# A windowed-attention layer that divides its probabilities before they are transposed, with the sink as one more column of the score bank

## The reference

```python
s = where(valid, q @ k.T * scale, -inf)
m = maximum(max(s), sink)
p = exp(s - m)
p = p / (sum(p) + exp(sink - m))
o = p @ v                       # then oc = o * silu(gate), and out = oc @ w_out
```

## Time and profile before

| | |
|---|---|
| median of 3 runs | 1123.61 us (1123.01 to 1125.2) |
| the profiled execution, its own time | 1122.13 us |
| its span in the profile | 1120.3 us |
| mean granted clock of TensorE | 0.997 |
| PE busy | 1088.0 us, 97% of the span |
| DVE busy | 967.9 us, 86% |
| ACT busy | 679.0 us, 61% |
| DMA queue of SP | 102.87 MB, 33.5% of 16 engines |

### The profile page before, as it was taken

One profiled execution on the slowest core, in us unless ns is written; L12 is line 12 of the kernel. 1 busy time (PEld: TensorE's weight loads), 2 busy tenths in 40 slices (PEclk: granted clock), 3 DMA queues, 4 the chain that ended last, 5 costly groups with the idle time before them and its releaser, 6 DMA issues. The chain is left out here.

```text
span 1120.3 us, 18456 instructions
## 1 busy us (share of the span) xinstructions
PE 1088.0 (97%) x5672; PEld 907.7 (81%) x5672; DVE 967.9 (86%) x1955; ACT 679.0 (61%) x1310; POOL 0.2 (0%) x4
## 2 busy tenths in 40 slices
PE   7999999999999999999999999999999999999996
PEld 6778778878888888888888867787888888888875
DVE  5879889889889889889889898789888988988886
ACT  6475565565654654654654765366677666677764
POOL 0000000000000000000000000000000000000000
PEclk9999999999999999999999999999999999999998
DMA  7614423323324224225125120454332324323111
GB/s 230 167 41 108 137 76 77 112 75 90 98 75 101 86 75 116 71 75 130 57 75 146 43 75 28 117 146 107 102 94 56 94 60 120 103 75 94 57 38 76
DMA packets 131530, 103.67 MB, mean 93 GB/s; under 512 B 5408, under 2 KB 116384, under 8 KB 131488
## 3 DMA queue, kind: packets, MB, share of 16 engines
q1 hardware_dynamic: 131344, 102.87, 33.5%
q10 hardware_dynamic: 144, 0.26, 0.1%
HBM read 77.95 MB, written 2.10 MB: 71 GB/s over the span
## 5 line engine op out<-in xcount | busy, mean ns | idle before, releaser
L74 PE MATMUL bank_proj<-hH,w_hi 128*128 128x512 f32 x856 | 341.1, 398 | 1.9 <-DVE w_lo L1295 1.1
L76 PE MATMUL bank_proj<-hH,w_lo 128*128 128x512 f32 x856 | 334.3, 390 | 0.0
L75 PE MATMUL bank_proj<-hL,w_hi 128*128 128x512 f32 x856 | 334.1, 390 | 0.0
L76 PEld LDWEIGHTS bank_proj<-hH,w_lo 128*128 128x128 f32 x856 | 160.7, 188 | 34.8
L74 PEld LDWEIGHTS bank_proj<-hH,w_hi 128*128 128x128 f32 x856 | 161.0, 188 | 33.2 <-DVE w_lo L1295 1.9
L75 PEld LDWEIGHTS bank_proj<-hL,w_hi 128*128 128x128 f32 x856 | 161.1, 188 | 30.1 <-issue 0.2
L2055 ACT ACTIVATE probs<-probs,small 128x256 f32<-128x256 f32 (+1 forms) x128 | 70.9, 556 | 53.2 <-DVE small L2314 52.9
L1295 DVE TENSOR_TENSOR w_lo<-w_raw,w_hi 128x1024 fp32r<-128x1024 f32 x74 | 89.6, 1219 | 0.8 <-ACT w_hi L764 0.7
L2062 ACT ACTIVATE probsT<-bank_odd_turn 128x256 fp32r<-128x256 f32 (+1 forms) x128 | 48.8, 433 | 64.7 <-PE bank_odd_turn L1778 64.3
L764 ACT ACTIVATE w_hi<-w_raw 128x1024 fp32r<-128x1024 f32 x74 | 77.9, 1053 | 0.2
L829 ACT ACTIVATE probs<-bank_score,small 128x512 f32<-128x512 f32 x64 | 43.4, 684 | 49.5 <-DVE small L1118 42.2
(11 more groups left out here) (456 smaller groups left out, 2148.2 us busy)
## 6 DMA issues: line engine op xcount, KB each, us to landing
w_raw<-in_w_in_even SPq DMA_DIRECT2D x72, 512.0 KB, 5.0
w_raw<-in_w_in_odd SPq DMA_DIRECT2D x36, 512.0 KB, 4.5
qs<-parts SPq DMA_DIRECT2D x96, 128.0 KB, 2.3
ks<-parts SPq DMA_DIRECT2D x40, 256.0 KB, 4.3
o_raw<-in_w_out_even SPq DMA_DIRECT2D x15, 512.0 KB, 6.2
o_raw<-in_w_out_odd SPq DMA_DIRECT2D x14, 512.0 KB, 6.4
mixT<-in_x SPq DMA_DIRECT2D x2, 512.0 KB, 5.9
attT<-in_x SPq DMA_DIRECT2D x2, 512.0 KB, 6.7
```

Of the source, the lines that this page charges most:

```text
L74: pe.matmul(out, hi, moving_hi, start=start, stop=False)
L75: pe.matmul(out, hi, moving_lo, start=False, stop=False)
L76: return pe.matmul(out, lo, moving_hi, start=False, stop=stop)
```

## The change

The sink gets a column of its own: before tile 0 of a half-step, `take_sinks` writes the sink logit (times 8, because the scores in the bank are not yet scaled) into column 384 of each score bank, and the scores of a tile are written so that they end at that column. `maxima` and `soft_max` then work on one column more, and the row sum of `soft_max` contains the sink. `weigh` becomes one reciprocal of two columns for each tile, directly behind the exponentials of that tile, and a new `divide` on ACT multiplies the two heads' probabilities by it in place. `turns` waits for `divide` now. The tile `spread`, the transposes of it, `apply_weight`, the shift and the exponential of the sink go away, and with them the pair versions in the last half-step. `highest` is a constant 1e30. The mask `band` grows from 384 to 642 columns, so that it has the extra column for each of the three kinds of tile.

```diff
@@ PE
             def scores(h, half, t):
                 if t == 0:
                     pe.wait_ge(q_moved.sem, q_moved.at(h, 4 * half))
+                    pe.wait_ge(sink_taken.sem, sink_taken.at(h, 2 * half + 2))
...
-                    at, query = S[a][:, 0:n * P], qs[:, half, a, t * P:(t + 1) * P]
+                    at, query = S[a][:, (3 - n) * P:3 * P], qs[:, half, a, t * P:(t + 1) * P]
...
                 scores(h, half, 1)
-                turn_weight(h_before, before, turn_of(half, True))
                 proj(h, n + 1, 0, 4)
@@ ACT
             def soft_max(h, half, t):
...
-                                   accum_out=row_sum[:, i:i + 1]).then_inc(softened[a].sem, 1)
+                                   accum_out=row_sum[:, i:i + 1]).then_inc(exped[a].sem, 1)
+            def divide(h, half, t):
+                _, n = window(t)
+                act.wait_ge(weighed.sem, weighed.at(h, tile_use(half, t)))
+                for a in range(2):
+                    i, at = 8 * half + 2 * t + a, probs[:, t % 2, a, 0:n * P]
+                    act.activation(at, at, ACT.Copy, scale=weight[:, i:i + 1]).then_inc(softened[a].sem, 1)
@@ ACT, half_step
                 soft_max(h, half, 0)
                 if not first:
-                    spread_weight(h_before, before)
                     swap_halves(h_before, before, 1)
+                divide(h, half, 0)
+                if not first:
                     if zeroth:
                         silu(0, 1, 0)
                     silu(h_before, 4 - 2 * half, half)
...
                     high(h, 6)
+                divide(h, half, 1)
                 if outs:
                     high_y(h - 1, 1)
                 high_turn(h, half, 1)
                 soft_max(h, half, 2)
                 swap_halves(h, half, 0)
+                divide(h, half, 2)
                 high_turn(h, half, 2)
                 soft_max(h, half, 3)
-                exp_sink(h, half)
+                divide(h, half, 3)
@@ DVE
             def take_sinks(h, half):
-                dve.tensor_copy(lowest[:, half], neg_sink[:, bass.ds(2 * KT * half + 2 * h, 2)]).then_inc(lowered.sem, 1)
+                for a in range(2):
+                    if S[a].free.due(h, 4 * half):
+                        dve.wait_ge(S[a].free.sem, S[a].free.at(h, 4 * half))
+                    dve.tensor_copy(S[a][:, 3 * P:3 * P + 1],
+                                    raised_sink[:, bass.ds(2 * KT * half + 2 * h + a, 1)]).then_inc(sink_taken.sem, 1)
...
-            def weigh(h, half):
+            def weigh(h, half, t):
+                i = 8 * half + 2 * t
                 for a in range(2):
+                    dve.wait_ge(exped[a].sem, exped[a].at(h, tile_use(half, t)))
+                dve.reciprocal(weight[:, i:i + 2], row_sum[:, i:i + 2]).then_inc(weighed.sem, 1)
@@ DVE, half_step
                     low(h, 4)
                 elif not first:
                     low_out(h - 1, 0)
+                weigh(h, half, 0)
+                if not half and not first:
                     low_out(h - 1, 1)
                     low_y(h - 1, 0)
...
                 if first:
                     part(0, -1)
                     rotate(0, 0)
                 else:
-                    apply_weight(h, before, use)
-                    scale_y(h_before, before, h, use)
+                    scale_y(h_before, before, h)
+                weigh(h, half, 1)
                 if not zeroth:
                     rotate(h, 2 * half + 1)
                     part(h, 2 * half + 1)
...
                 elif zeroth:
                     rotate(0, 3)
                     part(0, 3)
                 out(0)
+                weigh(h, half, 2)
...
                 if not zeroth:
                     maxima(h, half, 3)
+                take_sinks(h + half, 1 - half)
                 out(2)
-                shift_sink(h, half)
+                weigh(h, half, 3)
@@ the mask
-    band = np.concatenate([np.where(k >= q, 0.0, MASKED), 0.0 * (q + k), np.where(k <= q, 0.0, MASKED)], 1).astype(f32)
+    left, none, right = np.where(k >= q, 0.0, MASKED), 0.0 * (q + k), np.where(k <= q, 0.0, MASKED)
+    band = np.concatenate([left, none, right, none[:, :1], left, none, none[:, :1]], 1).astype(f32)
```

More of the change, by code:

```diff
@@ L1635, in tile_use @@
             return NC * half + t + 1
-        def turn_of(half, steady):
-            return 3 * half + 1 if steady else 6
         block = ctx.enter_context(nc.Block())
@@ L1795, in values @@
                     mm.then_inc(O.full.sem, 1)
-            def turn_weight(h_before, before, use):
-                if W.free.due(h_before + before, use - 1):
-                    pe.wait_ge(W.free.sem, W.free.at(h_before + before, use - 1))
-                pe.wait_ge(spread_out.sem, spread_out.at(h_before, before + 1))
-                for t in range(NC):
-                    mm = pe.transpose(W[:, t * P:(t + 1) * P], spread[:, 2 * t:2 * t + 2].rearrange("p a f -> p (a f)"),
-                                      eye[:])
-                mm.then_inc(W.full.sem, 1)
             def out_tile(h, j):
@@ L2063, in high_turn @@
                                    ACT.Copy).then_inc(probs_high[a].sem, 1)
-            def spread_weight(h, half):
-                act.wait_ge(weighed.sem, weighed.at(h, 2 * half + 2))
-                act.activation(spread[:], weight[:, 8 * half:8 * half + 8].unsqueeze(2).broadcast_to([P, 2 * NC, HD]),
-                               ACT.Copy).then_inc(spread_out.sem, 1)
             def swap_halves(h, half, i):
@@ L2079, in high_y @@
                 act.wait_ge(scaled_y.sem, scaled_y.at(h, half + 1))
-                act.wait_ge(W.full.sem, W.full.at(h, 6))
+                act.wait_ge(W.full.sem, W.full.at(h, 4))
                 act.activation(y[:, half, 0], gated[:, half], ACT.Copy).then_inc(y_high.sem, 1)
-            def exp_sink(h, half):
-                act.wait_ge(sink_shift.sem, sink_shift.at(h, half + 1))
-                at = weight[:, 8 * half:8 * half + 8]
-                act.activation(at, at, ACT.Exp).then_inc(sink_exp.sem, 1)
             def silu(h, n, half):
@@ L2313, in maxima @@
                     dve.sem_inc(mask_go.sem, 1)
-                    dve.tensor_tensor_reduce(out=probs[:, t % 2, a, 0:n * P], in0=S[a][:, 0:n * P],
-                                             in1=band[:, at:at + n * P], scale=-SCALE, scalar=lowest[:, half, a:a + 1],
+                    dve.tensor_tensor_reduce(out=probs[:, t % 2, a, 0:n * P + 1], in0=S[a][:, (3 - n) * P:3 * P + 1],
+                                             in1=band[:, at:at + n * P + 1], scale=-SCALE, scalar=highest[:],
                                              op0=ALU.add, op1=ALU.min,
@@ L2414, in half_step @@
                 before, h_before = 1 - half, (h if half else h - 1)
-                first, use = zeroth and not half, turn_of(half, not zeroth)
+                first = zeroth and not half
                 out = lambda j: zeroth or add_out(h, 4 * half + j)
@@ L2422, in half_step @@
                     rotate(0, -1)
-                if not first:
-                    weigh(h_before, before)
                 if half:
@@ L2461, in half_step @@
                 if not zeroth:
-                    scale_gate(h, 2 * half + 2, 1 - half, use)
+                    scale_gate(h, 2 * half + 2, 1 - half)
                 add_halves(h, half, 0)
@@ L2535, in gate_pair @@
                                   ALU.mult).then_inc(pair_gated.sem, 1)
-            def weight_pair(p):
-                dve.wait_ge(W.full.sem, W.full.at(HEADS - 1, 7 + p))
-                dve.wait_ge(pair_gated.sem, pair_gated.at(0, p + 1))
-                dve.tensor_tensor(gated[:, 1, pair(p)], gated[:, 1, pair(p)], W[:, pair(p)],
-                                  ALU.mult).then_inc(W.free.sem, 1)
             def low_pair(p):
```

146 lines of the change are left out of this document (43 added, 103 removed).

## The result

The changed kernel takes **1147.83 us** (median of 4 runs, 1146.05 to 1152.46) against 1123.31 (4 runs, 1122.53 to 1125.2): a ratio of 1.0221, 95% interval 1.0205 to 1.0237, slower. The forecast was 1145 in a range of 1131 to 1154.

The account below looks back on a forecast made before the run. The prediction took PE, busy 97% of the span, as the bound; 10.8 us (heads 1 to 6) + 8.5 (first head) + 2.5 (last head) = 21.8 us more gave 1145 us, range 1131 to 1154.

Parts of the forecast that it names:

- PE full, 0.9 us of room at tile 2: PE is busy 97% of the span; only 0.9 us lie between tile 2's exponentials and its turns.
- What goes: 0.35 us a half-step, 5.6 us: On PE the four weight transposes go: 0.35 us a half-step, 5.6 us over 16 sets.
- Divide pair 1.13 us, reciprocal 0.16, sink copies 0.16 each: New work: a 384-column divide pair on ACT 1.13 us, on DVE each reciprocal 0.16 and each sink copy 0.16.
- Steady half-step 0.9: In heads 1 to 6 each of 12 half-steps loses 0.9 us, 10.8 us in all, mostly at tile 2's turns.
- `y` and tile 1 about 0.1: In half 0 of a steady half-step, `y` and tile 1 come only about 0.1 us late.
- `weigh(1)` then holds `rotate` on DVE: In half 1, tile 1's reciprocal holds rotate for 0.63 us; idle time takes up 0.45, about 0.12 stays.
- 0 elsewhere: Sign in the middle half-steps: PE idles 0.9 to 1.3 us ahead of tile 2's turns and nowhere else.
- First head 8.5: In the first head, reciprocals queued behind rotary work on DVE make PE 8.5 us late after head 1's scores.
- rival E: PE's clock falls behind long new waits in the first and last heads, 2 us more each: 1149; chance 0.05.
- Last head 2.5: The last head loses 2.5 us, including 0.9 in half 0; the last half-step's divide(0) waits for swaps behind `values`.
- A: Rival: at tile 2's turns the relief wins, PE loses 5.6 us of work, 1118 us, faster; chance 0.07.
- D: Rival: slow divides and sink copies make tile 3 late too, 1.4 us a half-step, 1155 us; chance 0.07.

Follow-up runs that it names:

- e5_tile2: The changed kernel with tile 2's divides alone reading the mask and writing an unread tile, its turns waiting for the exponentials: 1139.16 us.
- e3_nodivide: The changed kernel without its reciprocals and divides, the probabilities staying undivided and turns waiting for the exponentials: 1112.01 us.
- e6_inside: The changed kernel with tile 1's reciprocal put behind the first multiply of rotate on DVE, in all but the first head: 1138.97 us.
- e12_aside_inside: e4_aside with tile 1's reciprocal also moved inside rotate, as in e6_inside: 1125.29 us.
- e2_swap: The changed kernel with tile 2's divides ahead of both swaps on ACT in every half-step: 1162.24 us.
- e9_split: e6_inside with one swap on each side of tile 2's divides on ACT and out(1) ahead of add_halves on DVE: 1141.23 us.
- e8_pool: The changed kernel with the second head's divide of each tile on GpSimd: 1155.97 us.
- e11_outfirst: e2_swap with out(1) also ahead of add_halves on DVE: 1154.46 us.
- e1_early: The changed kernel with the first head's reciprocals of tiles 0 to 2 moved ahead on DVE, before the rotary work: 1144.55 us.
- e4_aside: The changed kernel with all divides reading the mask and writing an unread tile, turns waiting for the exponentials: 1134.49 us.
- e10_best: e9_split with the reciprocal moves of e1_early, and the divides ahead of the swaps in the last half-step: 1137.78 us.

## Why the prediction was right, and where it wasn't

- **PE full, 0.9 us of room at tile 2.** The place is right: the turns of tile 2 wait in every steady half-step, and e5_tile2 shows that its divides alone are worth 0.31 us in each of them, although the next wait comes up behind.
- **What goes: 0.35 us a half-step, 5.6 us.** Mis-sized: 0.60 and 11.3 us (e3_nodivide). The start of the transposes to the next start is 0.35, but the matmuls behind them also take 2.84 us instead of 2.76. In half 0 there is more: the first output tile starts 1.03 us behind the scores ahead of it, 0.25 more than in half 1, because it waits for `y`. In e3_nodivide this 0.25 is gone, and half 0 gains 0.76, half 1 only 0.44. The multiply by the weight stood ahead of `rotate` and so ahead of `y`; that it was the reason is read off the order on DVE, no run takes it out alone. The text had seen that wait and priced only PE's own instructions.
- **Divide pair 1.13 us, reciprocal 0.16, sink copies 0.16 each.** Right: 1.12, 0.163 and 0.159. (By the Trainium skill, "ScalarE: Activation LUTs", section "What ACT_TABLE_LOAD costs", an ACTIVATE with one pointer operand takes about 280 ns + 0.833 ns a column, an estimate of 600 for 384; the trace has 605 on the mean, and agrees.)
- **Steady half-step 0.9.** The sum is right (0.88), its parts are not. Tile 2 was forecast at 0.81 and 0.83; PE's wait there is 0.87 in half 1 but 0.44 in half 0. The step that failed is "In half 0 ... `y` and tile 1 about 0.1", with "`weigh(1)` then holds `rotate` on DVE ... for 0.63 us ... about 0.12 stays" before it. Of the idle 0.53 and the 0.17 of the reciprocal nothing is taken up in half 0, because `low_y` ends the same queue: PE waits 0.83 for `y`, and the sign "0 elsewhere" fails there. e6_inside and e12_aside_inside put that place at 0.57 us a half-step, about 8 of the 24.5 us. Forecast: two half-steps 50.3; measured: 50.31. The forecast gain was too small by 0.25 a half-step and the forecast cost by about as much (1.25 against 1.48), so that the sum fits this well is luck.
- **First head 8.5.** Right in mechanism, and nearly in size. Measured from the first scores, the turns of tile 1 in half 0 come 4.8 us late (forecast 4.9 where they end), those of tile 2 8.2 (forecast 6.7), the last ones 12.0 (forecast 8.9). What is missing is the clock, 0.90 and 0.68 behind the longest wait:

```profile
734.00:738.00 4.00, 2.01 (x11) 1.82 (x12) 2.15 (x5) 2.34 (x5) 0.00 (x0) 0.90 0.99 221
738.00:742.00 4.00, 4.00 (x14) 3.16 (x13) 3.47 (x9) 1.31 (x4) 0.00 (x0) 0.68 0.54 140
```

  e2_swap has the same waits of 2.8 and 2.7 us and no fall of the granted clock in this head, so the two can be laid side by side. From the turns of tile 1 to those of tile 2 the change takes 8.29 us (735.99 to 744.28), of which 6.78 are left without its wait of 1.51. e2_swap takes 6.23, and 5.21 without its wait of 1.02:

```profile
735.94 1.05 PE L1774 MATMUL bank_odd_turn<-eye,probs 128*128 128x128 f32 x6 [2.79 <-ACT probs L2038]
...
742.17 1.06 PE L1774 MATMUL bank_odd_turn<-eye,probs 128*128 128x128 f32 x6 [1.02 <-ACT probs L2038]
```

  The first fall costs 1.57 us. The second, behind the wait at 771.55, costs 1.15 by the same comparison (6.11 to the next turns, against 4.96). Without these 2.7 us the head would lose 9.3 where 8.9 was forecast. That is rival E's mechanism, beside the forecast's, and its sign (a granted clock under 1) is there; the text gave it a chance of 0.05, and five of the seven profiles with this wait show it (last section).
- **Last head 2.5.** 3.8. The divide of the last half-step's tile 0 waits behind swaps for `values`, as forecast; PE waits 1.40 us there, and the clock falls to 0.58 behind it. No run takes this head's 3.8 us apart.
- **The rivals.** A is refuted as a forecast, though the relief was twice what it assumed. D's place (tile 3 late) has no idle time of PE in the change, only turns that take 0.45 and 0.53 us instead of 0.36; it is the next limit behind tile 2 (e5_tile2, e9_split).

## What to carry to other kernels

An instruction that waits is priced by what is queued behind it up to the first thing that the full engine waits for: a reciprocal of 0.17 us, put one instruction too early, cost about 8 of 24.5 us, and moving it by one multiply gave them back. A removed instruction can be worth more than its own time where it stands on a chain that the full engine already waits for. A wait that is removed may only uncover the one behind it, as tile 3 behind tile 2. To separate "more work" from "a longer chain", run the new work at its place without anybody waiting for it; here that split the loss of a half-step 0.84 to 0.69, where the sum alone had looked right. And look at each half-step before taking their mean: one of the twelve held a clock fall of 1.6 us.

## What the runs showed of the hardware

The granted clock of PE does not always fall after the same wait. Behind a wait of 2.8 us ahead of tile 1 in the first head it was 0.90 and 0.68 in two stretches of 4 us in the change, and 1.00 in both in e2_swap. Of the seven profiles with that wait (the change, e2_swap, e5_tile2, e6_inside, e8_pool, e9_split, e11_outfirst) five have a fall behind it and two, e2_swap and e5_tile2, have none; a fall costs 1.3 to 1.6 us up to the next turns. Here is e2_swap:

```profile
734.00:738.00 4.00, 2.06 (x13) 1.78 (x14) 2.16 (x5) 2.29 (x5) 0.00 (x0) 1.00 0.99 220
738.00:742.00 4.00, 3.15 (x17) 2.53 (x15) 3.43 (x9) 1.81 (x5) 0.00 (x0) 1.00 0.54 140
```

(By the Trainium skill, "TensorE: Matmul & The Clock Gate", section "HAM oscillation — how this bites in real kernels", idle gaps between bursts throttle the engine; the trace agrees in one of these two runs.)

The first microseconds of a program can differ as much as an edit is worth. From 12 us on, matmuls of 512 columns start 0.43 us apart in the change's profile and 0.23 in before's, although the clock column says 1.00 in both. The change:

```profile
12.24 0.63 PE L75 MATMUL bank_proj<-hL,w_hi 128*128 128x512 f32 x1
12.67 0.63 PE L76 MATMUL bank_proj<-hH,w_lo 128*128 128x512 f32 x1
```

The kernel before:

```profile
11.99 0.39 PE L75 MATMUL bank_proj<-hL,w_hi 128*128 128x512 f32 x1
12.22 0.39 PE L76 MATMUL bank_proj<-hH,w_lo 128*128 128x512 f32 x1
```

The slow spacing ends at 16.9 us in the change's profile and had ended by 10.5 in before's. That makes 2.6 of the 3.96 us that the odd layer starts late; most of the rest comes between 648 and 664 us, where the clock is 0.89 against 1.00. The edit touches neither: with the same even layer, e6_inside and e9_split start the odd layer 0.1 and 0.3 us ahead of before, and e1_early, e2_swap, e4_aside, e8_pool, e10_best, e11_outfirst and e12_aside_inside 2.6 to 3.9 us behind it. One profiled execution is to be compared from the place where the edit begins.
